# The low halves of all dense weight tiles move from GpSimd to VectorE

## The reference

```
h  = rms_norm(x);  z = h @ w_in            # c_q, c_kv, k_rope, dq, dk, dv, gates
q  = rms_norm(c_q) @ w_uq; kv = rms_norm(c_kv) @ w_ukv   # 16 latent heads
o_mla  = softmax(q k^T) v                  # rope, head norms on q and k
o_diff = (softmax(q1 k1^T) - lam softmax(q2 k2^T)) vd    # 8 heads, alibi bias
x  = x + (sigmoid(ga) * o_mla + sigmoid(gb) * o_diff) @ w_out
x  = x + expert_choice_moe(rms_norm(x))    # 16 experts, 32 tokens each, ff 2048
# second block
z  = rms_norm(x) @ w_in_2                  # short conv, 8 stick-breaking heads, spatial gating
x  = x + mix @ w_out_2
x  = x + relu(rms_norm(x) @ w_ff1)**2 @ w_ff2            # ff 4096
x  = x + sigmoid(rms_norm(x) @ w_ple_gate) * (p @ w_ple_proj)
```

## Time and profile before

| | |
|---|---|
| median of three runs | 1635.23 us |
| the profiled execution, own time | 1634.58 us |
| its span (first to last instruction) | 1632.8 us |
| TensorE busy | 1258.3 us (77%) |
| VectorE busy | 517.2 us (32%) |
| ScalarE busy | 393.5 us (24%) |
| GpSimd busy | 432.9 us (27%), 403.4 us of it on L492 |
| mean granted TensorE clock | 0.84 |

### The profile page before, as it was taken

One profiled execution on the slowest core, in us unless ns is written; L12 is line 12 of the kernel. 1 busy time (PEld: TensorE's weight loads), 2 busy tenths in 40 slices (PEclk: granted clock), 3 DMA queues, 4 the chain that ended last, 5 costly groups with the idle time before them and its releaser, 6 DMA issues.

```text
span 1632.8 us, 20334 instructions
## 1 busy us (share of the span) xinstructions
PE 1258.3 (77%) x8444; PEld 814.9 (50%) x8444; DVE 517.2 (32%) x769; ACT 393.5 (24%) x619; POOL 432.9 (27%) x222
## 2 busy tenths in 40 slices
PE   7786888887677577667667767757757977999997
PEld 7675667764233223323413423422322665899885
DVE  4678867441001000000100101000000658479305
ACT  4353654330000010010000000000000456455433
POOL 5575244320000000000000000000000654689886
PEclk8898999878866867877786777777878988999999
DMA  7343211459999999999999999999999634355550
GB/s 253 129 157 127 78 65 78 176 203 422 428 426 429 430 427 428 430 428 427 429 429 427 429 429 428 427 429 429 428 428 429 226 93 153 129 188 194 186 200 33
DMA packets 56300, 493.31 MB, mean 302 GB/s; under 512 B 6658, under 2 KB 7996, under 8 KB 31676
## 3 DMA queue, kind: packets, MB, share of 16 engines
q1 hardware_dynamic: 55308, 491.61, 74.1%
q10 hardware_dynamic: 944, 1.05, 0.2%
HBM read 491.59 MB, written 1.05 MB: 302 GB/s over the span
## 4 chain that ended last, share of the span: by engine, by line
PE 44%; DMA 34%; DVE 14%; issue 3%; ACT 3%; SPq 1%; POOL 0%; DVEq 0%; ACTq 0%
DMA ring<-in_expert_w_down 16%; DMA arena<-in_expert_w_down 16%; PE ps L1477 10%; PE ps L1786 9%; PE ps L1770 7%; PE ps L1521 6%; PE ps L1482 5%; PE ps L1802 3%; DMA ring<-in_w_in 2%; DVE xs L1299 2%; PE ps L1810 1%; DVE stat L923 1%; DVE stat L1181 1%; DVE stat L1054 1%; DVE stat L924 1%
## 5 line engine op out<-in xcount | busy, mean ns | idle before, releaser
L492 POOL TENSOR_TENSOR w_split<-ring,w_split 128x1024 fp32r<-128x1024 f32 (+3 forms) x178 | 403.4, 2276 | 1148.1 <-ACT w_split L568 1138.3
L568 ACT ACTIVATE w_split<-ring 128x1024 fp32r<-128x1024 f32 (+3 forms) x178 | 173.5, 986 | 193.2 <-PE ps L1482 137.0
L1786 PE MATMUL ps<-arena 128*32 128x512 f32 x1024 | 153.8, 748 | 60.1 <-DMA arena<-in_expert_w_up 59.6
L1786 PE MATMUL ps<-ring,arena 128*32 128x512 f32 x1024 | 156.6, 762 | 55.2 <-DMA ring<-in_expert_w_up 55.2
L1295 DVE TENSOR_TENSOR arena<-arena,ps 128x512 f32<-128x512 f32 x16 | 11.0, 687 | 426.8 <-PE ps L1786 426.8
L1299 DVE TENSOR_TENSOR xs<-ps,xs 128x512 f32<-128x512 f32 x64 | 39.7, 683 | 321.4 <-PE ps L1810 321.4
L1770 PE MATMUL ps<-onehot,xn_hi 128*128 128x32 f32 x256 | 94.4, 370 | 44.1 <-DVE onehot L1280 44.0
L1802 PE MATMUL ps<-arena 128*32 128x256 f32 x1024 | 90.3, 515 | 47.6 <-DMA arena<-in_expert_w_down 42.3
L1786 PEld LDWEIGHTS ps<-arena 128*32 128x32 f32 x1024 | 33.8, 128 | 172.5 <-DMA arena<-in_expert_w_up 93.3
L1786 PEld LDWEIGHTS ps<-ring,arena 128*32 128x32 f32 x1024 | 33.9, 130 | 170.0 <-DMA ring<-in_expert_w_up 87.7
L1477 PE MATMUL ps<-w_split,hT_hi 128*128 128x512 f32 (+1 forms) x320 | 96.9, 419 | 25.5 <-ACT w_split L568 18.7
(11 more groups left out here) (329 smaller groups left out, 1689.2 us busy)
## 6 DMA issues: line engine op xcount, KB each, us to landing
arena<-in_expert_w_gate SPq DMA_DIRECT2D x32, 2048.0 KB, 36.1
ring<-in_expert_w_up SPq DMA_DIRECT2D x32, 2048.0 KB, 36.4
arena<-in_expert_w_down SPq DMA_DIRECT2D x32, 2048.0 KB, 29.6
ring<-in_expert_w_gate SPq DMA_DIRECT2D x32, 2048.0 KB, 35.9
arena<-in_expert_w_up SPq DMA_DIRECT2D x32, 2048.0 KB, 35.6
ring<-in_expert_w_down SPq DMA_DIRECT2D x32, 2048.0 KB, 29.1
ring<-in_w_ff SPq DMA_DIRECT2D x32, 1024.0 KB, 5.0
ring<-in_w_in SPq DMA_DIRECT2D x24, 1024.0 KB, 5.0
```

What stands on the lines that cost most here:

```text
L492: ins = pool.tensor_tensor(buf[:, 1, :], w, buf[:, 0, :].bitcast(F32), ALU.subtract)
L568: act.activation(w_split[:, n % WBUFS, 0, 0:cols], slot_view(slot, cols)[:, n % 2, :], ACT.Copy).then_inc(split_hi, 1)
L1786: m = pe.matmul(ps[j * CAP:(j + 1) * CAP, bank, :], xe[:, kt, :], w[:, r, j * FCOL:(j + 1) * FCOL], start=kt == 0, stop=kt == KT - 1, skip ...
```

## The change

`low_parts` is taken from GpSimd's list and written into VectorE's, one or a few tiles at a time between its other instructions. GpSimd keeps its masks, the ten products L516 to L544, and two at the end. The slot of the ring is free when VectorE has made both low halves (`split_lo`), so `chunk_split` goes. The first five chunks are issued by SyncE ahead of all the small vectors (before: three), and the rows of small vectors stand between the loads of chunks 5, 6 and 7. Some work moves with it: ScalarE makes both squares of the first norm; the latent c is transposed after four dq tiles (before: six); the reading of PSUM is spread between low halves; the position buffers lie elsewhere. The core of the diff:

```diff
@@ sync
-                    sp.wait_ge(chunk_split, i - DENSE_SLOTS + 1)
+                    sp.wait_ge(split_lo, 2 * (i - DENSE_SLOTS + 1))
...
-            load(0)
-            load(1)
-            load(2)
+            for i in range(DENSE_SLOTS):
+                load(i)
...
+            load(DENSE_SLOTS)
+            load_rows(0, 4)
+            load(DENSE_SLOTS + 1)
+            load_rows(4, len(ROW_VECS))
+            load(DENSE_SLOTS + 2)
@@ gpsimd
-            for name in ("c", "dq", "uq0", "uq1", "ukv0", "ukv1", "dk", "dv", "gate_a"):
-                low_parts(name)
-            low_parts("gate_b", 0, 4)
...
-            for name, *_ in SECOND_BLOCK:
-                low_parts(name)
@@ vector
+            def low_parts(name, k0=0, k1=None):
+
+                cols = COLS[name]
+                for kt in range(k0, TILES[name] if k1 is None else k1):
+                    n = TILE0[name] + kt
+                    w = slot_view(n // 2 % DENSE_SLOTS, cols)[:, n % 2, :]
+                    buf = w_split[:, n % WBUFS, :, 0:cols]
+                    dve.wait_ge(split_hi, n + 1)
+                    dve.tensor_tensor(buf[:, 1, :], w, buf[:, 0, :].bitcast(F32), ALU.subtract).then_inc(split_lo, 1)
...
+            low_parts("dv", 2, 3)
+            roots(ss_d, rstd_d, 2 * HEADS, DQK)
+            low_parts("dv", 3, 4)
+            diff_scale(dk)
+            low_parts("dv", 4, 5)
...
+                if i < KT:
+                    low_parts("gate_a", i, i + 1)
+                if i == DHEADS:
+                    low_parts("gate_b", 0, 2)
...
+            gate_b_after = {1: 2, 2: 3, 4: 4, 6: 5, 8: 6, 10: 7}
+            out_after = {12: 0, 14: 1, 16: 2}
...
+                if i in gate_b_after:
+                    low_parts("gate_b", gate_b_after[i], gate_b_after[i] + 1)
...
+                for f in range(4 * p + 3, 4 * p + 7):
+                    name = ("conv", "cuv", "out2")[f // KT]
+                    low_parts(name, f % KT, f % KT + 1)
...
                 dve.wait_ge(f_ready, k + 1)
+                low_parts(following, 3 + j, 4 + j)
+                if j == 3 and b < 3:
+                    low_parts(following, 7)
+                    low_parts(f"up{b + 2}" if b < 2 else "down", 0, 3)
+            low_parts("down", 7)
+            low_parts("gate2", 0, 3)
             for h in range(HALVES):
                 half_complete(dve, "down", h)
@@ tensor
-            tiles("dq", hT, range(0, 6))
+            tiles("dq", hT, range(0, 4))
```

More of the change, by code:

```diff
@@ L644, in _ @@
             squares(0, dq.rearrange("p h d -> p (h d)"), sq)
+            high_parts("uq1", 1)
+            high_parts("ukv0", 0, 1)
+            evac("uq0", (q[:, 0, 0:768], whole))
             high_parts("ukv0", 1)
@@ L976, in _ @@
             dve.wait_ge(vec_ready, 1)
-            low_stage("attn", 0, "attn_norm_w")
+            low_parts("c", 0, 1)
+            low_stage("attn", 0, "attn_norm_w", range(0, 2))
+            for kt in range(1, KT - 1):
+                low_parts("c", kt, kt + 1)
+                low_stage("attn", 0, "attn_norm_w", [kt + 1])
+            low_parts("c", KT - 1)
             dve.wait_ge(x_loaded, 16)
-            norm(0, rstd_0, scaled=False)
+            norm(0, rstd_0, scaled=False, squared=True)
+            low_parts("dq", 0, 1)
             dve.wait_ge(vec_done, 2)
@@ L1084, in rope, with ukv_half @@
                        sin_t.unsqueeze(2).to_broadcast(full), *rope_t, third=third)
-            diff_sums(0)
+            def ukv_half(i):
+                heads = slice(i * HEADS // 2, (i + 1) * HEADS // 2)
+                evac(f"ukv{i}", (kf[:, 1, :].rearrange("p (n d) -> p n d", d=QK)[:, heads, 0:NOPE],
+                                 lambda src: src.rearrange("p (n d) -> p n d", d=128)[:, :, 0:NOPE]),
+                     (v1[:, 1, :].rearrange("p (n d) -> p n d", d=VD)[:, heads, :],
+                      lambda src: src.rearrange("p (n d) -> p n d", d=128)[:, :, NOPE:128]))
+            diff_sums(0)
+            low_parts("uq1", 1)
+            evac("uq0", (q[:, 1, 0:768], whole))
+            low_parts("ukv0", 0, 1)
+            evac("uq1", (q[:, 1, 768:1536], whole))
+            low_parts("ukv0", 1)
+            roots(ss_d, rstd_d, 2 * HEADS, DQK)
+            low_parts("ukv1", 0, 1)
+            ukv_half(0)
+            low_parts("ukv1", 1)
+            diff_scale(dq)
+            low_parts("dk", 0, 1)
+            ukv_half(1)
+            low_parts("dk", 1, 3)
             dve.wait_ge(lam_exp, 1)
@@ L1219, in _ @@
             low_stage("merge", 0, None)
+            low_parts("out", 3)
             def add_product(name):
@@ L1300, in _ @@
                                           ).then_inc(moe_added, 1)
-            low_stage("mix", 0, "norm1_g_2")
+            low_stage("mix", 0, "norm1_g_2", range(0, 2))
+            low_parts("qk2", 0, 1)
+            low_stage("mix", 0, "norm1_g_2", range(2, 4))
+            low_parts("qk2", 1, 2)
+            low_stage("mix", 0, "norm1_g_2", range(4, KT))
+            low_parts("qk2", 2, 3)
             dve.wait_ge(moe_added, 4 * EXPERTS + 4)
-            norm(2, scaled=False)
+            square_half()
+            low_parts("qk2", 3, 4)
+            norm(2, scaled=False, squared=True)
+            low_parts("qk2", 4, 5)
             for h in range(HALVES):
@@ L1401, in _ @@
                     gating_norm()
+                    low_parts("out2", 3, 4)
                 if p >= 1:
@@ L1413, in _ @@
             low_stage("ff", 4, "norm2_g_2")
+            low_parts("up0", 1, 3)
             dve.wait_ge(x_ready, 4)
-            norm(3, scaled=False)
+            square_half()
+            low_parts("up0", 3, 4)
+            norm(3, scaled=False, squared=True)
+            low_parts("up0", 4)
             step(dve.tensor_tensor(rstd_2, rstd_x, rstd_x, ALU.mult))
+            low_parts("up1", 0, 3)
             for k in range(4 * 4):
+                b, j = k // 4, k % 4
+                following = f"up{b + 1}" if b < 3 else "down"
                 dve.wait_ge(f_relu, k + 1)
@@ L1431, in _ @@
             dve.wait_ge(x_ready, 6)
-            norm(4, scaled=False)
+            square_half()
+            low_parts("gate2", 3, 4)
+            norm(4, scaled=False, squared=True)
+            low_parts("gate2", 4)
             dve.wait_ge(proj_out, 2)
@@ L1572, in _ @@
                 m.then_inc(cT_done, 1)
-            tiles("dq", hT, range(6, KT))
+            tiles("dq", hT, range(4, KT))
             pe.wait_ge(cT_lo, 2 * RT)
```

122 lines of the change are left out of this document (65 added, 57 removed).

## The result

The changed kernel takes 1584.54 us in the median of four runs (1583.97 to 1589.54) beside 1635.46 for the kernel before: ratio 0.9699, 95% interval 0.9687 to 0.971. The kernel before, run again beside every set of runs that follows, has medians of 1634.79 to 1635.51. The profiled execution is the fastest of the four (1583.97, span 1582.2).

The account below looks back on a forecast made before the run. Outside the weight-bound expert loop and TensorE-bound feed-forward, VectorE, stalled by GpSimd's low halves, was taken to hold TensorE. Stage gains less the small products' 1 and the tail's 3.7 sum to 30.4 us: 1605 us, range 1592 to 1623.

Parts of the forecast that it names:

- Start: First block to the first dq tile: five early chunks and VectorE's low halves gain 6.5 us, bounds 3 and 9.
- dq: First block's dq tiles: without stalls TensorE is last at 22.9 us, gain 11.2, bounds 6 and 12.
- Small products: First block after dq: TensorE full, VectorE rising to about 22 us, a tie; 1 us charged, bounds 0 and 4.
- Head norms: First block, 89 to 155.4 us: VectorE the bound at 52.9 us, 54 with waits; gain 12.4, bounds 6 and 14.
- Differential and latent heads: First block: differential heads no change, bounds +4 and -4; latent heads gain 3.3 us, bounds 0 and 8.
- The residue that I kept for the six products over dq: Latent heads: six products stay on GpSimd and still stall VectorE, put at 6 us.
- Second block's attention: Expert loop's end to feed-forward: earlier transposes, later turns, a wait gone at up0; together 1.7 us gained, bounds -4 and +8.
- The turns: Second block's attention, four turns after qk2's head norm: low halves ahead of the output's split lose 3.5 us.
- up0 and the tail: Second block: 1 us gained at up0's start; 3.7 lost behind `down`, where gate2 2's low half delays the addition.
- The slower one: Rival: low halves at the head of VectorE's list wait for TensorE; decides from 0.54 us each; 1647 us, chance 0.06.
- signs of being wrong: VectorE idle before L930 for ScalarE in the first block, or TensorE waiting for L930 instead of L1039, L1065, L1319.
- Everything goes through: Rival: upper bounds of start, dq, head norms and latent heads with the tail, 38 to 44 us, about 1593; chance 0.15.

## Why the prediction was wrong

The mechanism was right, and so was the sign: low halves on GpSimd hold VectorE, VectorE was on the path in the first block and not in the feed-forward, 41.5 of the 51 us hang on the engine alone, and GpSimd's added work brought the stall back. What failed is the sum, term by term of the table; the misses all lie on one side and add to 20. The plainest error is in the term of the head norms, where moved work was counted twice.

- *Start, 6.5 for 9.6.* I had VectorE make the last low half of c, the root and the low half of dq 0 after the end of c. The first two lay ahead of it, and the third began 0.4 us before it (c ends at 22.1), as the timeline of VectorE and TensorE in the changed kernel shows; TensorE waited 0.52 us. That neither the loads nor the missing stalls give this gain alone was not in the text.

```profile
21.50 0.16 DVE L902 SCALAR_TENSOR_TENSOR stat<-stat 128x2 f32<-128x2 f32 x1
21.69 1.23 DVE L930 TENSOR_TENSOR w_split<-ring,w_split 128x1024 fp32r<-128x1024 f32 x1
...
22.05 0.40 PE L1648 MATMUL ps<-ident,ffn_rows 4*128 4x4 f32 x2
...
23.16 1.20 PE L1566 MATMUL ps<-w_split,hT_hi 128*128 128x512 f32 x4 [0.52 <-DVE vec L977]
```

- *dq, 11.2 for 11.3.* Here TensorE was taken at the time of its tiles at full clock, and this is the term that held.
- *Small products, -1 for 1.1.* "TensorE was full" was read from busy time at a clock of 0.88. At 1.00 the same 97 products are 20.11 us. VectorE came to 19.99, near the 22 I had: the tie was there, and below the old length.
- *Head norms, 12.4 for 16.0.* This is the step that failed: I charged one reduction (2.3) and one root (2.9) to the small products and left them in the 52.9 of this stage as well, and missed that one scaling (2.3, L1065) had moved too. In the changed kernel reduction, root and 1.7 us of the scaling lie in the small products. 52.9 - 7.5 is 45.4; VectorE is busy 46.60. With 3.9 us in which it is idle (2.2 of them for ScalarE and TensorE), that makes 50.5. With its true load it is no longer alone at the limit: TensorE is busy 46.21.
- *Differential and latent heads, 3.3 for 8.6.* I costed the differential heads at nothing because VectorE's load stays (47.45 and 49.10 us busy). But the stage takes 51.6 to 51.8 us in all profiles with the first block's low halves on VectorE and 54.0 to 54.5 with them on GpSimd, where VectorE is busy less; so it is the stalls that cost it here, though no run shows which head's chain held one. In the latent heads TensorE's busy time fell by 4.0, of which the prediction had nothing. This stage scatters by 3.6 us in profiles of unchanged code, so its gain lies between 3.2 and 6.8, and the forecast of 3.3 isn't refuted there. The residue that I kept for the six products over dq was about right: the line that was L1181 still has 378 ns in the mean where its unhindered duration is 170.
- *Second block's attention, 0.7 without up0's wait for 6.3.* The head norms gave 5.6 for 4.2. The turns were charged 3.5 for low halves ahead of the split. The first turn lost as said (24.27 to 25.75 us, 1.5 for 1.3). The next two were charged 0.9 each and show 29.03 for 30.64 and 26.80 for 27.41. They scatter (28.54 to 30.39 and 25.22 to 26.88 over profiles of the same code there, so that they are shorter by 0.2 to 2.2 each), but none shows a loss: I had counted only one convolution of the stalls there. The run with the second block on GpSimd has the old lengths again (30.65, 27.41).
- *up0 and the tail, 1 for 1.3 and -3.7 for -3.7.* Both as written; the tail to 0.1 us, and its cause is shown by moving one low half.
- *The rivals.* The slower one did not come: from dq to the end of the latent heads VectorE was idle 0.5 us ahead of its low halves, and 8.9 before those of out, where TensorE waits for none of them: 0.17 over the 56, against the 0.54 from which it decides. One of the signs of being wrong did show in part: TensorE now waits for low halves, 4.3 us in the head norms, 2.5 in the differential heads and 8.0 in the second block's attention, where before it stood idle 7.42 for L1065 and 8.77 for L1319. It waits less than before in the first block, and in the second about as long. "Everything goes through", given 0.15, was the nearest, but its sum leaves out bounds that I had written: it takes 6 for the latent heads where the bound is 8, and nothing for the differential heads (4) and the second block (8). All the upper bounds of the stages, 9 + 12 + 14 + 4 + 8 + 8, with 2.5 lost at the tail, are 52.5, and the measured 51 lies below.

The range failed for the same reason, and start, small products and head norms came out above their own upper bounds (9.6 for 9, 1.1 for 0, 16.0 for 14). I took stalls out of VectorE's busy time and left TensorE's clock and the second order effects (a later stage that finds its input ready) at zero, and here both came out as gains. That they follow from the removed waits is what the stages suggest; no run separates them.

What stays open: how the 51 us divide between the stalls and the clock that follows them. Dummies in two waits of the kernel before show that a higher clock there gives nothing by itself, and no run here has the stalls removed and the clock held down.

## What to carry to other kernels

A long GpSimd instruction beside a VectorE that is on the path is paid for by the stage (here 1.7 us for each subtraction of 2.40, 0.6 for each copy of 1.05), even if nobody waits for its result; look for tiny VectorE instructions with the duration of a GpSimd one before moving anything else. When waits of the bound stage go, take TensorE's floor at full clock and book each moved instruction once, out of one stage and into the other. Work that an engine makes ahead of need belongs behind, not ahead of, the one addition that another engine waits for.

## What the runs showed that I had not expected

- A GpSimd copy with one input holds a two-input VectorE instruction as an addition with two does, for its 1.03 us; two engines alternating on 128x1024 take 6.06 and 5.71 us for what takes 2.44 and 4.8 apart.
- The granted clock at one place of one program (an idle 2.24 or 2.43 us of TensorE at the first latent head) held in one execution and fell in another, and that turn took 9.4 to 14.0 us over the profiles of kernels with the same code there. Behind the same idle 1.93 us in the last turns it fell in one profile and held in another. Single runs of the changed kernel spread over 7 us. A gain of 2 us in this stage, read from one profile of each kernel, says nothing until more profiles of the unchanged code are beside it.
- 28 and 34 dummy products in two waits of 7 us raised TensorE's clock around them and changed the time by less than 0.2%.
